# One kernel of a three-block transformer: how a head's values are multiplied with the turned attention map

## The reference

```python
# first block, 8 heads of 64: causal, with a slope per head (both blocks of 256 keys are always seen)
s = jnp.einsum('bhqd,bhkd->bhqk', q, k) * 64 ** -0.5 - slope * dist
s = jnp.where(kpos <= qpos, s, NEG)
out = jnp.einsum('bhqk,bhkd->bhqd', jax.nn.softmax(s), v)
...
# second block, layer 0, 8 heads of 128 values: difference of two softmaxes, all keys
pr = jax.nn.softmax(s, axis=-1).reshape(B, H, 2, DIFF_Q_BLOCK, S)
a = (pr[:, :, 0] - lam_full * pr[:, :, 1]).astype(v.dtype)
o = jnp.einsum('bhqk,bkhe->bqhe', a, v)
...
# second block, layer 1, 16 query heads of 64: keys at most 128 positions away, and a sink
mask = (jnp.abs(kpos - qpos) <= WINDOW) & (kpos >= 0) & (kpos < S)
pr = e / (jnp.sum(e, axis=-1, keepdims=True) + jnp.exp(sink - m))
o = jnp.einsum('bnhgqc,bnchd->bnqhgd', pr.astype(v.dtype), vb)
```

## Time and profile before

| | |
|---|---|
| median of 3 runs (lowest, highest) | 1975.0 us (1973.26, 1975.79) |
| span of the profiled execution, first to last instruction | 1972.9 us |
| PE busy | 1940.0 us, 98% |
| DVE busy | 1188.4 us, 60% |
| ACT busy | 924.4 us, 47% |
| POOL busy | 1109.2 us, 56% |
| matmuls of linear layers (L393 to L395, 128x512) | 7584 of 9232 |

### The profile page before, as it was taken

How to read it: one execution, slowest core, us unless ns; L and a number is a source line. 1 busy time by engine, 2 the same in 40 slices (tenths; PEclk the granted TensorE clock), 3 DMA queues, 4 the chain that set the end, 5 groups by cost and what they waited for, 6 DMA issues and landing times.

```text
span 1972.9 us, 25163 instructions
## 1 busy us (share of the span) xinstructions
PE 1940.0 (98%) x9232; PEld 1590.0 (81%) x9232; DVE 1188.4 (60%) x1952; ACT 924.4 (47%) x1740; POOL 1109.2 (56%) x842
## 2 busy tenths in 40 slices
PE   8999999999999999999999999999999999999997
PEld 6877888888888877777888888888777888888886
DVE  6773325353433488877675646856688675746855
ACT  5653336533333366555453433445477543443443
POOL 5345544454444456454576665755785576666662
PEclk9999999999999999999999999999999999999998
DMA  4122233232232321111322222223110323222321
GB/s 160 65 70 96 89 114 128 95 104 102 97 111 94 111 98 68 45 65 54 128 103 100 97 96 97 97 90 109 65 54 33 128 97 107 97 86 96 107 93 57
DMA packets 52106, 182.72 MB, mean 93 GB/s; under 512 B 5776, under 2 KB 6160, under 8 KB 51984
## 3 DMA queue, kind: packets, MB, share of 16 engines
q1 hardware_dynamic: 51984, 181.12, 26.4%
HBM read 174.80 MB, written 6.29 MB: 92 GB/s over the span
## 4 chain that ended last, share of the span: by engine, by line
PE 92%; DVE 5%; ACT 1%; issue 1%; DMA 0%; POOL 0%; SPq 0%; DVEq 0%; ACTq 0%; POOLq 0%
PE b L393 28%; PE b L395 28%; PE b L394 28%; PE b L415 2%; PE b L407 1%; PE b L448 1%; PE b L439 1%; PE b L438 1%; DVE sm L574 1%; PE b L408 1%; PE b L409 1%; DVE ra L621 1%; DVE fa L586 0%; PE b L426 0%; DVE ra L483 0%
## 5 line engine op out<-in xcount | busy, mean ns | idle before, releaser
L239 POOL TENSOR_TENSOR ra<-raw,ra 128x512 fp32r<-128x512 f32 x632 | 883.2, 1405 | 771.7 <-ACT ra L283 770.0
L393 PE MATMUL b<-ra 128*128 128x512 f32 x2528 | 1000.7, 396 | 15.9 <-POOL ra L239 9.4
L395 PE MATMUL b<-ra 128*128 128x512 f32 x2528 | 985.9, 390 | 0.0
L394 PE MATMUL b<-ra 128*128 128x512 f32 x2528 | 985.2, 390 | 0.0
L283 ACT ACTIVATE ra<-raw 128x512 fp32r<-128x512 f32 x632 | 392.8, 628 | 531.9 <-PE b L395 526.4
L393 PEld LDWEIGHTS b<-ra 128*128 128x128 f32 x2528 | 475.5, 188 | 121.2 <-issue 15.2
L395 PEld LDWEIGHTS b<-ra 128*128 128x128 f32 x2528 | 475.0, 188 | 101.0
L394 PEld LDWEIGHTS b<-ra 128*128 128x128 f32 x2528 | 475.7, 188 | 93.3
L737 DVE TENSOR_TENSOR h<-b,h 128x512 f32<-128x512 f32 x136 | 91.8, 683 | 61.4 <-PE b L395 60.6
L628 DVE TENSOR_TENSOR tmp<-b,rb 128x512 f32<-128x512 f32 x62 | 42.4, 689 | 100.2 <-PE b L395 100.0
L621 DVE TENSOR_TENSOR ra<-b,ra 128x512 fp32r<-128x512 f32 (+4 forms) x166 | 91.9, 567 | 17.6 <-ACT ra L334 14.8
(11 more groups left out here) (276 smaller groups left out, 1900.4 us busy)
## 6 DMA issues: line engine op xcount, KB each, us to landing
raw<-in_f_g SPq DMA_DIRECT2D x40, 512.0 KB, 3.5
raw<-in_f_v SPq DMA_DIRECT2D x40, 512.0 KB, 3.5
raw<-in_f_d SPq DMA_DIRECT2D x40, 512.0 KB, 3.5
raw<-in_w_up SPq DMA_DIRECT2D x32, 512.0 KB, 3.5
raw<-in_w_down SPq DMA_DIRECT2D x32, 512.0 KB, 3.5
raw<-in_p_g SPq DMA_DIRECT2D x16, 512.0 KB, 3.5
raw<-in_w_gp SPq DMA_DIRECT2D x8, 512.0 KB, 3.4
raw<-in_w_ga SPq DMA_DIRECT2D x8, 512.0 KB, 3.4
```

What stands on the lines that cost most here:

```text
L239: e.tensor_tensor(wl, src, wh.bitcast(F), ALU.subtract).then_inc(*w_low.mark(n))
L393: e.matmul(ps, wh[:, c:c + 128], xh, start=start, stop=False)
L394: e.matmul(ps, wh[:, c:c + 128], xl, start=False, stop=False)
L395: last = e.matmul(ps, wl[:, c:c + 128], xh, start=False, stop=stop)
```

## The change

All three attentions now multiply a key block's values with the turned map of all query blocks that see it at once: up to 512 columns of bank 6. The turned map lies in one buffer of four key blocks by 512 queries for each part. The causal and the differential attention have one row of products per head, for key blocks 0 to 3. The sliding one has two (`part_groups`): key blocks 1 and 0, then 2 and 3. The widths: causal 512, 384, 256, 128 (before 256, 128 and 256, 256, 256, 128); differential four times 512 (before eight times 256); sliding 384, 256 and 384, 256 (before 256, 256, 128, twice). Each width stands for two matmuls, in the differential attention for three. A row waits for the low parts of all blocks that it reads: all four, in the sliding attention blocks 0 to 2 and then 1 to 3. A block of the next head is turned only after the last row that reads this block (`last_reader`): the head's one row, or in the sliding attention the first row for block 0 and the second for 1 to 3. The assumed price of a product follows its width.

```diff
@@ tensor_program
         elif kind == "pv":
-            (vh, vl), pt, pr, parts, b, ready = a
+            (vh, vl), pt, parts, b, ready = a[:5]
             for t in ready:
                 w.wait_ge(*t)
-            first = True
-            for k, (_, kt, lo, hi) in enumerate(parts):
+            for k, (kt, lo, hi) in enumerate(parts):
                 vs = slice(128 * kt, 128 * kt + 128)
                 ph, pl = (pt[z][:, kt, lo:hi] for z in range(2))
-                dst = m.banks[b][:, 256 * pr + lo:256 * pr + hi]
-                e.matmul(dst, vh[:, vs], ph, start=first, stop=False, skip_group_check=True)
+                dst = m.banks[b][:, lo:hi]
+                e.matmul(dst, vh[:, vs], ph, start=k == 0, stop=False, skip_group_check=True)
...
         elif kind == "pv_halves":
-            v, pt, pr, parts, b, ready = a
+            v, pt, parts, b, ready, begins, ends = a
...
-                e.matmul(dst, both, pt[0][:, kt, lo:hi], start=k == 0, stop=False, skip_group_check=True)
-                x = e.matmul(dst, both, pt[1][:, kt, lo:hi], start=False, stop=k == len(parts) - 1, skip_group_check=True)
+                e.matmul(dst, both, pt[0][:, kt, lo:hi], start=begins and k == 0, stop=False, skip_group_check=True)
+                x = e.matmul(dst, both, pt[1][:, kt, lo:hi], start=False, stop=ends and k == len(parts) - 1,
+                             skip_group_check=True)
@@ duration
-            return sum((3 if kind == "pv" else 2) * (0.109 if hi - lo == 128 else 0.12) for _, _, lo, hi in a[3])
+            return sum((3 if kind == "pv" else 2) * max(0.109, 0.0133 + (hi - lo) / 2400.0) for _, lo, hi in a[2])
@@ heads
+    def part_groups(seen):
+
+        if all(len(x) == 4 for x in seen) or len(seen[0]) == 4:
+            return [[0, 1, 2, 3]]
+        return [[1, 0], [2, 3]]
...
-        pt = [[m.ra[:, PTb + 2 * p + z, :, :].rearrange("p a (b c) -> p (a b) c", b=2)
-               for z in range(2)] for p in range(2)]
+        pt = [m.ra[:, PTb + 2 * z:PTb + 2 * z + 2, :, :].rearrange("p a b c -> p (a b) c") for z in range(2)]
+        seen = [[i for i in range(4) if span(i)[0] <= 128 * kt < span(i)[1]] for kt in range(4)]
+        groups = part_groups(seen)
+        last_reader = [max(g for g, kts in enumerate(groups) if any(i in seen[kt] for kt in kts)) for i in range(4)]
...
-            free = (used[(t - 1, i // 2)],) if t and i % 2 == 0 else ()
+            free = (used[(t - 1, last_reader[i])],) if t else ()
...
-                    if (t, i) not in p_done or bank_free[tbk[0]] is None or (t and (t - 1, i // 2) not in used):
+                    if (t, i) not in p_done or bank_free[tbk[0]] is None or (t and (t - 1, last_reader[i]) not in used):
...
-            for pr in range(2):
+            for g, kts in enumerate(groups):
+                blocks = sorted({i for kt in kts for i in seen[kt]})
...
-                    return (*VT(t)[-1], small[(t, 2 * pr)], small[(t, 2 * pr + 1)], *(bank_free[obk] or ()))
-                yield rank0(t) + per * (2 * pr + 2), "pe", need
+                    return (*VT(t)[-1], *(small[(t, i)] for i in blocks), *(bank_free[obk] or ()))
+                yield rank0(t) + per * (blocks[-1] + 1), "pe", need
...
-                for kt in range(4):
-                    qs = [i for i in (2 * pr, 2 * pr + 1) if span(i)[0] <= 128 * kt < span(i)[1]]
-                    if qs:
-                        parts.append((-len(qs), kt, 128 * (qs[0] % 2), 128 * (qs[-1] % 2) + 128))
-                parts.sort()
+                parts = [(kt, 128 * seen[kt][0], 128 * seen[kt][-1] + 128) for kt in kts]
+                begins, ends = g == 0, g == len(groups) - 1
```

More of the change, by code:

```diff
@@ L417, in tensor_program @@
         elif kind == "pv":
-            (vh, vl), pt, pr, parts, b, ready = a
+            (vh, vl), pt, parts, b, ready = a[:5]
             for t in ready:
                 w.wait_ge(*t)
-            first = True
-            for k, (_, kt, lo, hi) in enumerate(parts):
+            for k, (kt, lo, hi) in enumerate(parts):
                 vs = slice(128 * kt, 128 * kt + 128)
                 ph, pl = (pt[z][:, kt, lo:hi] for z in range(2))
-                dst = m.banks[b][:, 256 * pr + lo:256 * pr + hi]
-                e.matmul(dst, vh[:, vs], ph, start=first, stop=False, skip_group_check=True)
+                dst = m.banks[b][:, lo:hi]
+                e.matmul(dst, vh[:, vs], ph, start=k == 0, stop=False, skip_group_check=True)
                 e.matmul(dst, vh[:, vs], pl, start=False, stop=False, skip_group_check=True)
                 x = e.matmul(dst, vl[:, vs], ph, start=False, stop=k == len(parts) - 1, skip_group_check=True)
-                first = False
             x.then_inc(*pv.mark(n))
         elif kind == "pv_halves":
-            v, pt, pr, parts, b, ready = a
+            v, pt, parts, b, ready, begins, ends = a
             for t in ready:
                 w.wait_ge(*t)
-            for k, (_, kt, lo, hi) in enumerate(parts):
-                dst = m.banks[b][:, 256 * pr + lo:256 * pr + hi]
+            for k, (kt, lo, hi) in enumerate(parts):
+                dst = m.banks[b][:, lo:hi]
                 both = v[:, 256 * kt:256 * kt + 128]
-                e.matmul(dst, both, pt[0][:, kt, lo:hi], start=k == 0, stop=False, skip_group_check=True)
-                x = e.matmul(dst, both, pt[1][:, kt, lo:hi], start=False, stop=k == len(parts) - 1, skip_group_check=True)
+                e.matmul(dst, both, pt[0][:, kt, lo:hi], start=begins and k == 0, stop=False, skip_group_check=True)
+                x = e.matmul(dst, both, pt[1][:, kt, lo:hi], start=False, stop=ends and k == len(parts) - 1,
+                             skip_group_check=True)
             x.then_inc(*pv.mark(n))
@@ L1244, in lows @@
         def lows(t, i, b, nb, k0, turned):
-            h0 = 128 * (i % 2)
-            dst = [pt[i // 2][z][:, k0:k0 + nb, h0:h0 + 128] for z in range(2)]
+            dst = [pt[z][:, k0:k0 + nb, 128 * i:128 * i + 128] for z in range(2)]
             src = banks[b][:, 0:128 * nb].rearrange("p (a b) -> p a b", b=128)
-            free = (used[(t - 1, i // 2)],) if t and i % 2 == 0 else ()
+            free = (used[(t - 1, last_reader[i])],) if t else ()
             yield 0, "ac", lambda: (turned, *free)
@@ L1273, in products_of @@
         def products_of(t):
-            for pr in range(2):
+            for g, kts in enumerate(groups):
+                blocks = sorted({i for kt in kts for i in seen[kt]})
                 def need():
-                    if (t, 2 * pr) not in small or (t, 2 * pr + 1) not in small or VT(t) is None:
+                    if VT(t) is None or any((t, i) not in small for i in blocks):
                         return None
-                    if pr == 0 and bank_free[obk] is None:
+                    if g == 0 and bank_free[obk] is None:
                         return None
-                    return (*VT(t)[-1], small[(t, 2 * pr)], small[(t, 2 * pr + 1)], *(bank_free[obk] or ()))
-                yield rank0(t) + per * (2 * pr + 2), "pe", need
+                    return (*VT(t)[-1], *(small[(t, i)] for i in blocks), *(bank_free[obk] or ()))
+                yield rank0(t) + per * (blocks[-1] + 1), "pe", need
                 *values, vt = VT(t)
-                ready = (*vt, small[(t, 2 * pr)], small[(t, 2 * pr + 1)])
-                if pr == 0:
+                ready = (*vt, *(small[(t, i)] for i in blocks))
+                if g == 0:
                     ready += tuple(bank_free[obk])
                     bank_free[obk] = None
-                parts = []
-                for kt in range(4):
-                    qs = [i for i in (2 * pr, 2 * pr + 1) if span(i)[0] <= 128 * kt < span(i)[1]]
-                    if qs:
-                        parts.append((-len(qs), kt, 128 * (qs[0] % 2), 128 * (qs[-1] % 2) + 128))
-                parts.sort()
+                parts = [(kt, 128 * seen[kt][0], 128 * seen[kt][-1] + 128) for kt in kts]
+                begins, ends = g == 0, g == len(groups) - 1
                 if len(values) == 1:
-                    x = row("pv_halves", values[0], pt[pr], pr, parts, obk, ready)
+                    x = row("pv_halves", values[0], pt, parts, obk, ready, begins, ends)
                 else:
-                    x = row("pv", values, pt[pr], pr, parts, obk, ready)
-                used[(t, pr)] = done("pe", "pv", x)
+                    x = row("pv", values, pt, parts, obk, ready, begins, ends)
+                used[(t, g)] = done("pe", "pv", x)
             heads_used.add(t)
-            launch(O(t, used[(t, 1)]))
+            launch(O(t, used[(t, len(groups) - 1)]))
             if t + 1 < n:
```

## The result

The changed kernel takes **1981.45 us** (median of 5 runs, 1980.07 to 1982.2) against 1974.98 us before (5 runs, 1973.26 to 1975.79). The ratio is 1.0036, with an interval of 1.0025 to 1.0047: slower by 6.5 us. The forecast was 1977.3, +2.3 us. Its sign held and its size did not: most of its chance, 0.63, lay on a time between 1971.0 and 1979.0, and slower than that had 0.27.

What follows compares the result with a forecast made beforehand. The prediction took TensorE to bound the kernel. Products -3.6, starved heads +5.2, causal and differential waits 0 and the sliding attention's end +0.7 gave +2.3 us on 1975.0, so 1977.3 us, range 1971.8 to 1982.0.

Steps and rivals of the forecast that it cites:

- The bound: Whole kernel: TensorE bounds it, in 92% of the chain of waits; whether it waits longer is decided in the attentions.
- The products, -3.6: All three attentions: fewer, wider matmuls save TensorE 0.65 us (causal), 0.96 (differential) and 1.95 (sliding).
- Causal and differential waits, 0: Causal and differential attention: linear steps or scores fill the longer chain, no net wait; bounds -0.9 and +1.0 us.
- The starved heads, +5.2: Sliding attention: heads 7, 8, 12 and 13, with 0 to 2 linear steps, wait longer; bounds +2.5 and +7.7 us.
- End of the sliding attention, +0.7: First step needing the last head waits longer, by one linear step moved ahead of the last products; 0 to 1.2 us.
- Rivals: Four other outcomes for the whole kernel: 1971.7, 1982.6, 1986.6 and 1980.9 us, chances 0.17, 0.10, 0.05 and 0.06.
- rival 4: Products: a matmul costs only its columns, so the saving doesn't come; 1980.9 us, chance 0.06.
- rival 2: Sliding attention: the turned map's single buffer paces starved heads at 7.5 us each; 1982.6 us, chance 0.10.

Runs made afterwards that it cites:

- e4: The changed kernel plus six matmuls of 512 columns that nobody reads before block 3's turn in heads 7, 8, 12 and 13; 1976.59 us.
- e6: The changed kernel with the sliding attention's linear steps dealt out evenly, four or five each for heads 3 to 13; 1972.2 us.
- e2: The kernel before with the wide rows of products in the sliding attention alone; 1982.75 us.
- e1: The kernel before with the wide rows of products in the causal and differential attention alone; 1974.5 us.
- e3: The changed kernel with the sliding attention's linear steps held back to the dealing of the kernel before; 1973.95 us.

## Why the prediction was half right

- *The bound.* Right: TensorE, and the sliding attention as the place where it is decided.
- *The products, -3.6.* Right as a price. Added up over the timeline, the products take 0.72 us less in the causal attention (0.65 said), 1.66 less in the differential one (0.96 said; three of them had waited before) and 1.77 less in the sliding one with its clock whole (21.67 before, 19.90 in e4; 1.95 said). The estimate of 0.1735 us for 384 columns holds (0.17). By the Trainium skill ("TensorE: Matmul & The Clock Gate", "Back-to-back issue gap") 384 columns would take 384 / 2.4 + 2.5 = 162.5 ns, an estimate by its formula; the trace, with 0.17 to 0.18 us, lies nearer to the columns plus 15 ns.
- *Causal and differential waits, 0.* Wrong for the causal attention: it came out 0.48 us longer instead of 0.65 shorter. The forecast had looked for waits at the products; here turns wait, the one at 119.97 for VectorE. With the 0.5 us gained beyond the forecast in the differential attention the two together miss by +0.7, inside the bounds given. The start of this execution, 1.08 us shorter, hid it.
- *The starved heads, +5.2.* The waits are where the forecast put them, behind the same two masks. VectorE's timeline in head 7, to lay beside the earlier trace rows:

```profile
1478.85 0.69 DVE L611 TENSOR_TENSOR b<-b,ssq 64x512 f32<-64x512 f32 x1 [0.20 <-ACT ssq L307]
1479.46 0.54 DVE L598 CUSTOM_DVE_ANT_0 fa<-b,mask 128x385 f32<-128x385 f32 x1
...
1479.93 0.55 DVE L598 CUSTOM_DVE_ANT_0 fa<-b,mask 128x385 f32<-128x385 f32 x1
...
1480.41 1.61 DVE L620 TENSOR_TENSOR ra<-b,ra 128x384 fp32r<-128x384 f32 x3
```

  In three of the four TensorE is idle for 1.5 us or more as claimed (1.71, 1.71, 1.89), in head 12 only 1.34. As waits they cost what was said: e4's stretch less before's is 151.62 - 148.37 = 3.25, and with the 1.95 that the products save there, 5.2. Part of this agreement is luck. Head 7 had lost 0.63 us before, too (1480.77 - 1472.61 = 8.16 with five steps, for 4.12 + 3.42), which the forecast overlooked, and in e4 heads 4, 5, 9 and 11 lose 0.9 us together, which it didn't expect.
- **The step that failed** is this term's price. It took 1.75 to 2.55 us per starved head from head 13 of before, whose clock had stayed whole behind the wait, and reckoned every matmul behind a wait at the full clock. That "the granted clock is at its full level in every slice but the last" was read off 40 slices of 49 us, and even with three slow stretches that row doesn't change. The missing entry is +4.4 us for three falls of the clock, some 1.5 us each; e4 shows it by filling the waits.
- *End of the sliding attention, +0.7.* Wrong, and small: with one step less ahead of it the wait is 0.83 for 0.92, since the need comes 1546.07 - 1542.88 = 3.19 us after the last product and not 3.99 as in the earlier trace rows. I had taken that distance as fixed; the 0.7 came out 0. VectorE's timeline shows why it shrank. Before, `add_half` stood behind the residual of the linear step that follows the last product and started at 1538.30, 1.78 us after it; now that step stands ahead of the products, its residual is done sooner, and `add_half` starts at 1543.83, 0.95 us after the last product. The residual before, then now:

```profile
1537.58 0.69 DVE L737 TENSOR_TENSOR h<-b,h 128x512 f32<-128x512 f32 x1 [1.76 <-PE b L395]
...
1542.62 0.69 DVE L736 TENSOR_TENSOR h<-b,h 128x512 f32<-128x512 f32 x1 [0.95 <-PE b L395]
```

- *Rivals.* None came true. The measured 1981.45 lies close to rival 4 (1980.9) and rival 2 (1982.6), both for other reasons: the savings are real, and heads without slow clock take 5.6 to 7.4 us, not 7.5 each. A time that fits a rival doesn't prove it.
- *The sum.* By stretches of the two traces: -1.08 at the start, +0.48 causal, -1.43 differential, +7.62 sliding and -0.2 elsewhere, +5.4, which is span against span, 1978.3 - 1972.9. In the forecast's terms that is -3.6 + 5.2 + 0 + 4.4 = +6.0, and +0.7 for the two other attentions, less 1.3 that stand outside all three. Median against median it is +6.5. The last microsecond isn't assigned: each trace is one execution, and executions of one kernel differ by more.

## What to carry to other kernels

Where a tuned kernel waits for other engines, count the filling work that each wait has for cover, head by head, before and after: a change that only makes an operation wider can deal the same filler out otherwise, and between the change and e6 only that dealing was edited, 1981.45 against 1972.2 us, where the width itself saves an estimated 3.6. Price a wait of TensorE with what comes behind it as well, and read the granted clock in windows of a few us around it, not in the page's slices. If a wait can't be removed, matmuls that nobody reads can keep the clock up (e4: 4.4 us of sliding attention for 24 matmuls).

## What the hardware showed that I had not expected

- Waits of TensorE of 1.3 to 1.9 us were at times followed by a stretch of some us at the 1.2 GHz level, and 512 columns then start 0.43 us apart instead of 0.228. It isn't the length of the wait alone that decides: in the changed kernel it fell behind 1.34 us in head 12 and 1.71 in head 7, and not behind 1.71 in head 8, where it did behind 1.72 in e2. Behind 1.57 us it fell in e1 and not in the earlier trace rows, and behind 1.89 us in head 13 of the changed kernel and not in e3.
- The same order of instructions shows both outcomes. In e1 two heaps of runs are 2.5 us apart, of which one fall of the clock explains some 1.5. In the kernel before the split is not clear: 9 of its 27 runs in the first session have a mean clock of 0.996 (mean 1974.62) and 18 have 0.997 (mean 1973.85), but their times overlap. Another thing that comes and goes is the wait of 0.90 us of an early score, in the traces of e2, e4 and e6 alone. What decides from run to run stays open; no experiment here went after it.
- Filling the waits took the effect away in e4's trace, and its eleven runs point the same way: mean clock 0.996 or 0.997, with the same mean time to 0.2 us, against 0.993 to 0.995 in the five of the change.
